# A two-block transformer kernel: four stage borders, late turned masks and the decay row reordered

## The reference, cut to what matters

```python
# block 1
mod = silu(c) @ w_ada + b_ada;  shift, scale, gate = split(mod, 3)
h = rms_norm(x, g_pre) * (1 + scale) + shift
qa, ka, va, fa, za, qb, kb, vb, zb = split(h @ w_in)
oa = forgetting_attention(qa, ka, va, fa + b_fgate) * silu(za)   # s = q.k*scale + cum_q - cum_k
ob = sliding_window_sink_attention(rope(qb), rope(kb), vb, sinks) * silu(zb)
x = x + gate * rms_norm(concat(oa, ob) @ w_out, g_post)
# block 2, 16 meta tokens ahead of x
q_a, c_kv, q_idx, k_idx, w_idx, gate_a, q_h, f_h, i_h, gate_h = split(h @ w_in_2)
# index scores: sum over 4 heads of relu(q_idx . k_idx) * w_idx; causal; the top 256 keys of each query
s_idx = einsum('bqhk,bqh->bqk', relu(einsum('bqhd,bkd->bqhk', qi, ki) * 64**-0.5), wi)
a = attention of q_a over the selected latent keys, with relative bias, * silu(gate_a)
r = hgrn2(q_h, f_h, i_h, lb) normalised, * silu(gate_h)
h = layer_norm(DN_ALPHA * h + concat(a, r) @ w_out_2, ln_g, ln_b)
```

## Time and profile before

| | us |
|---|---|
| median of 3 runs | 3661.6 (3656.85 to 3664.55) |
| the profiled execution | 3664.95 (its span 3663.2) |
| busy PE / DVE / ACT / POOL in it | 3305.1 / 2020.6 / 1406.2 / 897.7 |
| mean granted TensorE clock in it | 0.954 of full |

### The profile page before, as it was taken

One profiled execution on the slowest core, in us unless ns is written; L12 is line 12 of the kernel. 1 busy time (PEld: TensorE's weight loads), 2 busy tenths in 40 slices (PEclk: granted clock), 3 DMA queues, 4 the chain that ended last, 5 costly groups with the idle time before them and its releaser, 6 DMA issues. The chain is left out here.

```text
span 3663.2 us, 43930 instructions
## 1 busy us (share of the span) xinstructions
PE 3305.1 (90%) x15840; PEld 2521.2 (69%) x15840; DVE 2020.6 (55%) x3695; ACT 1406.2 (38%) x2381; POOL 897.7 (25%) x836
## 2 busy tenths in 40 slices
PE   3899999899999997986789999997895999999798
PEld 3799888656666665875567787886783666666487
DVE  5211011266666666332389999975672555555466
ACT  4100001134444445211158999232553333333354
POOL 0121111356455450001321333434232111111000
PEclk9999999899999999997899999998997999999899
DMA  5231224465454433435211335454134423222344
GB/s 201 68 106 58 86 92 123 125 144 130 108 126 105 102 89 108 131 121 213 70 44 49 88 106 182 126 161 165 52 111 155 109 62 87 67 60 56 114 150 129
DMA packets 331914, 400.83 MB, mean 109 GB/s; under 512 B 100324, under 2 KB 249188, under 8 KB 319124
## 3 DMA queue, kind: packets, MB, share of 16 engines
q1 hardware_dynamic: 259256, 288.60, 28.3%
q10 hardware_dynamic: 67488, 78.03, 7.0%
q0 software_dynamic: 4960, 31.46, 3.1%
HBM read 265.39 MB, written 132.62 MB: 109 GB/s over the span
## 5 line engine op out<-in xcount | busy, mean ns | idle before, releaser
L2228 PE MATMUL f_pO<-f_PT,f_vv 128*128 128x512 f32 (+3 forms) x944 | 383.4, 489 | 24.7 <-ACT f_PT L2258 24.7
L2320 DVE TENSOR_REDUCE f_mxc<-f_pM 128x1 f32<-128x512 f32 (+2 forms) x448 | 240.1, 541 | 220.3 <-PE f_pM L2152 128.0
L2258 ACT ACTIVATE f_PT<-f_pS 128x512 f32<-128x512 f32 (+3 forms) x472 | 221.2, 472 | 353.0 <-PE f_pS L2191 172.5
L2325 DVE CUSTOM_DVE_ANT_0 n_junk<-n_pM,n_chosen 128x512 bf16<-128x512 f32 (+4 forms) x352 | 200.2, 571 | 271.0 <-PE n_pM L2158 137.8
L2670 PE MATMUL cbank<-hT_high,cw_hi 128*128 128x512 f32 x800 | 317.5, 397 | 29.8 <-POOL cw_lo L2623 23.6
L2860 DVE TENSOR_SCALAR_CACHE_REDUCE sharedI<-xI,TI 128x768 bf16<-128x768 f32 (+10 forms) x276 | 339.6, 1296 | 5.4 <-DVE TI L2865 5.2
L571 PE MATMUL p_bank<-hT_high,p_w_hi 128*128 128x512 f32 (+1 forms) x768 | 304.7, 397 | 33.0 <-POOL p_w_lo L537 27.5
L2258 ACT ACTIVATE n_PT<-n_pS 128x512 f32<-128x512 f32 (+4 forms) x352 | 177.4, 504 | 387.7 <-PE n_pS L2208 387.3
L2670 PE MATMUL cbank<-hT_low,cw_hi 128*128 128x512 f32 x800 | 314.7, 393 | 0.0
L2670 PE MATMUL cbank<-hT_high,cw_lo 128*128 128x512 f32 x800 | 314.6, 393 | 0.0
L2228 PE MATMUL n_pO<-n_PT,n_vv 128*128 128x512 f32 (+4 forms) x704 | 305.8, 516 | 0.0
(11 more groups left out here) (418 smaller groups left out, 7448.2 us busy)
## 6 DMA issues: line engine op xcount, KB each, us to landing
cw_raw<-in_w_in_dram SPq DMA_DIRECT2D x50, 512.0 KB, 4.7
f_zz<-scratch_z ACTq DMA_DIRECT2D x128, 128.0 KB, 3.0
p_w_raw<-in_w_in_dram SPq DMA_DIRECT2D x23, 512.0 KB, 3.8
lent<-scratch_qkb POOLq DMA_DIRECT2D x40, 256.0 KB, 10.7
scratch_z<-p_stage ACTq DMA_DIRECT2D x32, 256.0 KB, 2.4
scratch_qk_high<-p_stage ACTq DMA_DIRECT2D x32, 256.0 KB, 2.6
scratch_qk_low<-p_stage_low ACTq DMA_DIRECT2D x32, 256.0 KB, 3.2
f_vv<-scratch_vf SPq DMA_DIRECT2D x16, 512.0 KB, 14.3
```

The source lines that it names most:

```text
L2228: pe.matmul(pO[:, B % 2, c0:c1], lhsT=vv[0:nk, b, kt, :], rhs=PT[0:nk, u % PR, c0:c1], start=(kt == 0 and not heads[h].local), stop=(heads ...
L2258: act.activation(PT[0:nk, u % PR, c0:c1], pS[0:nk, u % SR, c0:c1], ACT.Exp, scale=0.125).then_inc(s_ex, 1)
L2320: v.tensor_reduce(to, pM[:, n % 2, 0:wd], AX.X, ALU.max).then_inc(s_mx, 1)
L2325: v.tensor_tensor_reduce(junk[:, n % 2, 0:wd], pM[:, n % 2, 0:wd], chosen[:, at:at + wd], 1.0, 3.0 * NEG, ALU.add, ALU.max, accum_out=to). ...
```

## The change

Modulation: squares and root of group 1 stand ahead of the product loop, those of group 2 within group 0 and of group 3 within group 1; DVE makes the diagonals of group 1 ahead of split 0, of group 2 after split 8, of group 3 after split 18. f_: SP loads the decay row after the first blanking, PE waits for the second. n_: ACT issues the turned masks of j = 1 to 3 after the first exponentials. Turning: SP loads the first index weights (512 KB) after metaT; POOL no longer waits for its stores, SP does at the end of p2. p2: the first tile by ACT and DVE as in p_; SP then loads selection's first weights into the same buffer `c_w_first`. Selection: ACT and DVE split these, SP loads tile 1's weights ahead of keys and w_T, POOL makes the memsets of `bits` later, and scores begin after product LATER = 3.

```diff
@@ -131,6 +131,8 @@
+        ROOT_AT = {6: 2, 2 * DC: 3}
...
         block = own.enter_context(nc.Block())
@@ -209,17 +211,18 @@
                     act.dma_start(turns[z][:, q * QB:(q + 1) * QB], trig[z][q * 32:q * 32 + 32]).then_inc(s_tst, 16)
-            for t in range(4):
-                square(t)
-            root(0)
+            for g in range(2):
+                for t in range(4 * g, 4 * g + 4):
+                    square(t)
+                root(g)
             act.wait_ge(s_mod, 1)
+            squares_at = {2 + z: 8 + z for z in range(4)} | {DC + 4 + z: 12 + z for z in range(4)}
             for n in range(NG * DC):
-                g, k = n // DC, n % DC
                 modulated(n)
-                if g < NG - 1 and 2 <= k < 6:
-                    square(4 * g + 2 + k)
-                if g < NG - 1 and k == 6:
-                    root(g + 1)
+                if n in squares_at:
+                    square(squares_at[n])
+                if n - 1 in ROOT_AT:
+                    root(ROOT_AT[n - 1])
             act.wait_ge(s_tst, 16 * 12)
@@ -309,12 +312,14 @@
             v.scalar_tensor_tensor(gain[:], mod[:, DC:2 * DC], 1.0, flat[:, 3 * DC:], ALU.add, ALU.mult).then_inc(s_mod, 1)
+            variance(1)
+            diagonals(1)
             for n in range(NG * DC):
                 split(n)
-                if n < (NG - 1) * DC and n % DC == 6:
-                    variance(n // DC + 1)
-                if n < (NG - 1) * DC and n % DC == 7:
-                    diagonals(n // DC + 1)
+                if n in ROOT_AT:
+                    variance(ROOT_AT[n])
+                if n - 2 in ROOT_AT:
+                    diagonals(ROOT_AT[n - 2])
@@ -513,7 +518,13 @@
                          (5, lambda: load_gate_rows(DC, b_ada[:, 2 * D:3 * D])), (5, lambda: load_gate_rows(DC + 1, g_post[:, :])))
+            if ahead is not None:
+                to, src, loaded = ahead
+                sp.wait_ge(s_split, 1)
+                sp.dma_start(to, src).then_inc(loaded, 16)
             sweep(sp, load, sides)
+            if stored is not None:
+                sp.wait_ge(stored, 64)
             if forget is not None:
@@ -963,7 +974,7 @@
-def stage_turn(nc, used, rows, meta, blocks, hT_meta, HT):
+def stage_turn(nc, used, rows, meta, blocks, hT_meta, HT, stored, ahead):
@@ -978,13 +989,14 @@
         s_m, s_const, s_gp = m.sem("t_meta_loaded"), m.sem("t_identity"), m.sem("t_pool_own")
-        s_st = m.sem("t_blocks_stored")
         s_mt, s_mh, s_ml = m.sem("t_meta_turned"), m.sem("t_meta_high"), m.sem("t_meta_low")
...
             sp.dma_start(mt[:], meta[:, :]).then_inc(s_m, 16)
+            to, src, loaded = ahead
+            sp.dma_start(to, src).then_inc(loaded, 16)
             with sp.Fori(0, NT // NB) as i:
@@ -1002,8 +1014,7 @@
                 for part in range(2):
-                    gp.dma_start(HT[part, b - 2], blocks[part][b][:].bitcast(F32)).then_inc(s_st, 16)
-            gp.wait_ge(s_st, 64)
+                    gp.dma_start(HT[part, b - 2], blocks[part][b][:].bitcast(F32)).then_inc(stored, 16)
@@ -1908,7 +1919,7 @@
                     if h < NB:
-                        sp.wait_ge(s_blank[b], 2)
+                        sp.wait_ge(s_blank[b], 1)
                     sp.dma_start(KA[b][HD:HD + 2, :].bitcast(F32), hd.cum).then_inc(s_cum[b], 16)
@@ -2139,6 +2150,8 @@
                     if hd.cum is not None:
+                        if h < NB:
+                            pe.wait_ge(s_blank[b], 2)
                         pe.wait_ge(s_cum[b], 16 * (h // NB) + 16)
@@ -2292,11 +2305,13 @@
             if rel is not None:
-                for j in range(NJ):
-                    load_turned_masks(j)
+                load_turned_masks(0)
             for u in steps():
...
                     exps(u)
+                    if rel is not None and u == 0:
+                        for j in range(1, NJ):
+                            load_turned_masks(j)
                 if turned_at(u) is not None:
@@ -2416,7 +2431,7 @@
     BITS = 32
-    RING, PER = 4, 8
+    RING, PER, LATER = 4, 8, 3
     PASSES = ((0, 0), (0, 1), (1, 0))
@@ -2437,9 +2452,9 @@
-        return range(min(NU, PER * p), min(NU, PER * (p + 1)))
...
-    SCORED = -(-NU // PER)
+        return range(min(NU, PER * max(0, p - LATER)), min(NU, PER * max(0, p - LATER + 1)))
...
+    SCORED = -(-NU // PER) + LATER
@@ -2480,9 +2495,10 @@
+    early, s_early = first_weights
     with ExitStack() as own:
         m = Memory(nc, own, used)
-        w_raw = m.sb("cw_raw", [P, 2, DC, P])
+        w_raw = [early, m.sb("cw_raw", [P, DC, P])]
         w_part = [[m.sb(f"cw_{n}{b}", [P, DC, P], F32R) for b in range(2)] for n in ("hi", "lo")]
@@ -2550,15 +2568,11 @@
         def _(sp):
-            sp.dma_start(w_T, KW[ID:ID + IH, :]).then_inc(s_in, 16)
-            for half in range(2):
-                sp.dma_start(k_raw[half * ID:(half + 1) * ID, :], KW[0:ID, :]).then_inc(s_kin, 16)
...
             def load_weights(n):
...
                 first = tiles[n][1].first
-                sp.dma_start(w_raw[:, n % 2], wv[:, :, first:first + P]).then_inc(s_raw[n % 2], 16)
+                sp.dma_start(w_raw[n % 2][:], wv[:, :, first:first + P]).then_inc(s_raw[n % 2], 16)
@@ -2579,8 +2593,10 @@
-            load_weights(0)
             load_weights(1)
+            for half in range(2):
+                sp.dma_start(k_raw[half * ID:(half + 1) * ID, :], KW[0:ID, :]).then_inc(s_kin, 16)
+            sp.dma_start(w_T, KW[ID:ID + IH, :]).then_inc(s_in, 16)
             for p, (n, q) in enumerate(products):
@@ -2607,20 +2623,19 @@
             own_.settle()
-            for r in range(1, BITS):
-                own_.up(gp.memset(bits[:, r:r + 1], 1 << (BITS - 1 - r)))
-            own_.settle()
             gp.sem_inc(s_const, 1)
...
                 b = n % 2
-                gp.wait_ge(s_raw[b], 16 * (n // 2) + 16)
+                gp.wait_ge(s_raw[b], 16 * (n // 2) + (16 if b else 0))
                 if n >= 2:
                     gp.wait_ge(s_prod, ends_tile[n - 2] + 1)
-                gp.tensor_copy(w_part[0][b][:], w_raw[:, b]).then_inc(s_hi, 1)
-                gp.wait_ge(s_hi, n + 1)
-                gp.tensor_tensor(w_part[1][b][:], w_raw[:, b], w_part[0][b][:].bitcast(F32), ALU.subtract
+                gp.tensor_copy(w_part[0][b][:], w_raw[b][:]).then_inc(s_hi, 1)
+                gp.wait_ge(s_hi, n)
+                if n == 1:
+                    gp.wait_ge(s_split, 1)
+                gp.tensor_tensor(w_part[1][b][:], w_raw[b][:], w_part[0][b][:].bitcast(F32), ALU.subtract
                                  ).then_inc(s_split, 1)
@@ -2635,19 +2650,22 @@
-            split_weights(0)
             gp.wait_ge(s_kin, 32)
...
             gp.wait_ge(s_ksplit, 2)
+            split_weights(1)
             for i in (FREE, FREE + 1):
                 split_queries(i)
-            split_weights(1)
+            for r in range(1, BITS):
+                own_.up(gp.memset(bits[:, r:r + 1], 1 << (BITS - 1 - r)))
+            own_.settle()
+            gp.sem_inc(s_bits, 1)
             ready = FREE + 2
             for n in range(2, len(tiles)):
-                while ready < NT and unit_end[ready - 2] < PER * ends_tile[n - 2]:
+                while ready < NT and unit_end[ready - 2] < PER * (ends_tile[n - 2] - LATER):
                     split_queries(ready)
@@ -2699,7 +2717,7 @@
                 product(p)
-                if p == 0:
+                if p == LATER:
                     pe.wait_ge(s_const, 1)
@@ -2775,11 +2793,13 @@
+            act.wait_ge(s_early, 16)
+            act.activation(w_part[0][0][:], early[:], ACT.Copy).then_inc(s_first, 1)
             for i in (FREE, FREE + 1):
...
                 take_product(p)
-                if p == 0:
+                if p == LATER:
                     act.wait_ge(s_ksplit, 2)
@@ -2817,6 +2837,8 @@
                 own_.settle()
+            v.wait_ge(s_first, 1)
+            v.tensor_tensor(w_part[1][0][:], early[:], w_part[0][0][:].bitcast(F32), ALU.subtract).then_inc(s_split, 1)
             v.wait_ge(s_wt, 1)
@@ -2860,6 +2882,7 @@
+            v.wait_ge(s_bits, 1)
             for r in range(BITS):
@@ -3001,15 +3024,23 @@
         hT_meta = [rows.enter_context(nc.sbuf_tensor(f"hT2_meta_{n}", [P, DC, NMETA], F32R)) for n in ("high", "low")]
+        m = Memory(nc, rows, used)
+        chosen_first = m.sb("c_w_first", [P, DC, P]), m.sem("c_first_weights_loaded")
         kept = [[rows.enter_context(t) for t in block_pair(b)] for b in range(2)]
...
             blocks = [[pair[part] for pair in both] for part in range(2)]
-            stage_turn(nc, used, X1, meta_tokens, blocks, hT_meta, HT)
+            index_first = chosen_first[0], m.sem("p2_weights_loaded")
+            blocks_stored = m.sem("t_blocks_stored")
+            wv2 = w_in_2[0].rearrange("(k p) n -> p k n", p=P)
+            stage_turn(nc, used, X1, meta_tokens, blocks, hT_meta, HT, blocks_stored,
```

(13 more changed lines are left out.)

## The result

The changed kernel took 3627.94 us in the median of four executions (3618.47 to 3628.97), the kernel before 3661.15 us in the same comparison; the ratio is 0.9903, with a 95% interval of 0.9888 to 0.9918. That is 33 us faster where 66 were forecast, and above the range's upper end of 3616. A later comparison, five executions against eleven of the kernel before, gave 0.9909 (0.9893 to 0.9925).

What follows compares the result with a forecast made beforehand. PE, working 90% of the span, was taken as the bound. Terms 19.2 + 2.2 + 19.0 + 14.0 + 11.0 = 65.4 us took the profiled 3664.95 to 3599.6, less 3.3 for the median: 3596 us, range 3584 to 3616.

Steps and rivals of the forecast that it cites:

- Modulation: Modulation: DVE's splits set the pace after product 6, its last split ends at 91.0; gain 19.2 us (17 to 21).
- The half-clock rival: Modulation: a product costs 1.71 us at half clock, gain 7 us instead of 19, total 3608; chance 7%.
- f_ start: Start of first attention: PE limited by DVE's last memset, ending at 712.35; gain 2.2 us (0 to 2.5).
- Turn to p2: Border from turning to index projection: first product at 1687.2 against 1706.22; gain 19.0 us (16 to 20.5).
- The rival that says just this: Turn to p2: stage end still holds POOL until its DMAs land; gain 3.3 us, total 3612; chance 8%.
- Selection: Start of key selection: fifth score unit at T + 31.6 (T: SP's first issue), three more products done; gain 14.0 us (8 to 15.5).
- keys land at about T + 10: Selection: keys land about 10 us after SP's first issue (T), tile 1's weights split by T + 20.2.
- Product 3 ends: Selection: product 3 ends at T + 25.6, T being SP's first issue in the stage.
- n_ start: Start of second attention: masks DVE awaits come 12.4 us earlier with turned masks issued later; gain 11 us (5 to 14).
- late masks: Second attention: turned masks of j = 1 queue behind head 1's loads; gain 3 instead of 11, total 3604; chance 15%.
- selection (3610): Selection gives its gain back if queries split late or masks end later than products; total 3610; chance 7%.
- the rival by which the removed rests cost clock: Whole kernel: dense stretches' granted clock falls, each 1% costing 33 us, kernel slower below a mean of 0.935; chance 2%.

Runs made afterwards that it cites:

- e5: The changed kernel with POOL's wait for its four stores put back at the end of turning; 3624.59 us.
- e2: The changed kernel with the four stores of turned blocks issued by ACT instead of POOL; 3612.43 us, ratio 0.9862.
- e4: The changed kernel with selection's two loads of keys issued ahead of tile 1's weights; 3622.02 us, ratio 0.9880.

## Why the prediction was wrong

The sum failed in three of its terms, which lack 13.9, 6.6 and 13.1 us; the other two are off by 2 and 1.4. By the prediction's own steps:

*Modulation:* -21.2 against -19.2, inside its bounds. The second batch of squares cost nothing, where 1.5 us were allowed: ACT's products, at a period of 0.69 us between the batches against DVE's 1.06, gave it lead enough. The half-clock rival did not come.

*f_ start:* 1.2 us instead of 2.2, of which the ledger keeps 0.8. The direction was right; PE still starts 1.1 us after the last memset's end, where the step let it start at once. The memset was to be the releaser and the profile names the row's load; what fills the 1.1 us is not shown.

*Turn to p2:* this is the step that failed most, by 13.9 us. "POOL's last instruction becomes the issue of the last store" was right of the code and wrong of the border: leaving the block, POOL drains, and that took 16.02 us. The rival that says just this was priced at 3.3 us (measured 5.1) and given 8%, with the argument that the wait is an instruction and goes. That argument was no evidence on what the border does. The 0.38 us DRAIN in the trace of before was none either, since it stood behind a wait that had done its work. e5 and e2 settle it.

*Selection:* -7.4 against -14.0. The step "keys land at about T + 10" was 11.9, with tile 1's weights now ahead of them, so PE rested 3.5 us instead of 1.6: 1.8 us late at the start of product 3. "Product 3 ends" took product 3 at full clock, where it ran mostly at half, 8.3 us instead of 5.4: 2.9 more. And from there to the fifth unit the step took 6.0 us by leaving out the 2.64 us for which PE waits for queries in the trace of before; it took 8.1, with a rest of 2.08: 2.1 more. The three put the fifth unit at T + 38.4 instead of 31.6, 6.8 us late, which is the 6.6 that the stage lacks at its end. The bound of 8 was missed by 0.6. DVE's slack at the end was there, 25 us where the step said some 29.

*n_ start:* +2.1 against -11. The step on the masks was right (11.4 us by the trace against 12.4; 8.7 to 12.3 over the six executions with this order), and the first scores come 33.4 us into the stage, as forecast. What failed is the last sentence of the step: turned masks wanted 8.5 us after the first scores and issued 2 us after them. The prediction had the landing times of these loads in its trace, 13 to 24 us in a full queue, and did not set them against those 6.5 us (the 0.95 MB of j = 1 landed 15.9 us after their issue, and PE was there 11.3 us after its first scores); it priced the rival at +8 instead of +13, without the half clock that follows the rest, and gave it 15%.

*What the rows before could have told.* The two largest misses had the same shape: a wait was removed or moved, and what ended last next was a transfer that the trace already showed. Rivals and forecast were also added as if at most one or two could miss; here three of five did. Nor did the range hold what was said of it: late masks (+8) together with the stores (3612) or with selection (3610) make 3620 and 3618 by the prediction's own prices, above its upper end of 3616.

*The slower side:* the mean granted clock rose from 0.954 to 0.959 in the profiled execution and to 0.956 to 0.958 in the others, so the rival by which the removed rests cost clock did not come.

## What to carry to other kernels

Taking a wait for POOL-issued stores off the end of a stage gains nothing if the stage's end drains POOL; give such stores to ACT or SP, and the border opens at once. A load moved out of a full queue has to be set against its landing time in that queue, not its size: move what is wanted last, keep what is wanted next. Where the same program's executions differ by 10 us in stretches that no edit touches, compare edits stretch by stretch, and do not add up a whole profile.

## What the runs showed of the hardware

- POOL's DRAIN at the end of a block lasted 16.02 us, until 1669.0, and the last of the DMAs that POOL had issued landed at 1668.8; when ACT or SP had just issued the same stores, their DRAIN lasted 0.15 and 0.12 us.
- Rests of PE of 3.5 us (selection) and 8.0 us (n_) were each followed by a stretch at the half clock (0.51 and 0.50), while 15 us of products with five pauses of 0.15 to 0.55 us kept 1.00. A rest was not needed for it: in e4 the clock fell to 0.50 at product 3 after 9.3 us in which PE was busy throughout, the last 2.4 of them with the meta product.
- One unchanged stretch of 620 us took 610.6 to 622.7 us over 13 executions of programs that have it in common, with 23.9 to 37.5 us of half clock in it; twice with the identical program, 612.4 and 622.7.
